# Two chunked scans of a hybrid transformer block: preparing the next tile during the levels of this one, beta in the decay, small blocks in the second scan's first levels

## The reference, cut to what matters

```python
# gated delta rule, per chunk (g: cumulated log decay)
decay = exp(where(incl, g[..., :, None] - g[..., None, :], -inf))
k_beta = k * beta[..., None]
a = where(strict, einsum('bhntd,bhnsd->bhnts', k_beta, k) * decay, 0.0)
rhs = concatenate([v * beta[..., None], k_beta * exp(g)[..., None]], -1)
sol = triangular_solve(a + eye(C), rhs, lower=True, unit_diagonal=True)   # -> u, w
qk = einsum('bhntd,bhnsd->bhnts', q, k) * decay
v_new = u - w @ S
o = (q * exp(g)) @ S + qk @ v_new
S = S * exp(g_last) + (k * exp(g_last - g)).T @ v_new

# second scan: the decay G is a vector over the 128 key features
dec = exp(where(tri, G[:, :, :, None, :] - G[:, :, None, :, :], -inf))
A = einsum('bhtd,bhsd,bhtsd->bhts', q, k, dec)
o = (q * exp(G)) @ S + A @ v
S = exp(G_last) * S + (k * exp(G_last - G)).T @ v
```

## Time and profile before

| | |
|---|---|
| median of 3 runs | 3026.27 us (3025.71 to 3035.88) |
| profiled execution | 3025.89 us, its span 3024.0 us |
| busy | PE 2452.7 us (81%), its weight loads 1330.1 (44%), DVE 1006.4 (33%), ACT 476.1 (16%), POOL 330.2 (11%) |
| mean granted clock of PE | 0.894 of full speed (2.4 GHz) |
| DMA | 540.71 MB, 179 GB/s over the span |
| first scan | about 555.7 to 850 us |
| second scan | about 2106 to 2349 us |

### The profile page before, as it was taken

How to read it: one execution, slowest core, us unless ns; L and a number is a source line. 1 busy time by engine, 2 the same in 40 slices (tenths; PEclk the granted TensorE clock), 3 DMA queues, 4 the chain that set the end, 5 groups by cost and what they waited for, 6 DMA issues and landing times. The chain is left out here.

```text
span 3024.0 us, 37725 instructions
## 1 busy us (share of the span) xinstructions
PE 2452.7 (81%) x15432; PEld 1330.1 (44%) x15432; DVE 1006.4 (33%) x2009; ACT 476.1 (16%) x942; POOL 330.2 (11%) x388
## 2 busy tenths in 40 slices
PE   5888998767679599999998696898466848898896
PEld 2346565667558222222222374567365632222221
DVE  0034432465635322222221308200768341212213
ACT  1213112211120100000000106202221110000000
POOL 0000000233300010011010000000356000000000
PEclk9999998677679799999999799999678879999997
DMA  7400114200042399999999211011000329999995
GB/s 257 157 28 22 29 42 166 100 2 2 3 146 98 115 339 348 346 339 341 346 356 358 70 48 65 28 56 56 0 1 1 140 77 389 409 409 410 409 410 235
DMA packets 165552, 540.71 MB, mean 179 GB/s; under 512 B 14512, under 2 KB 49712, under 8 KB 158896
## 3 DMA queue, kind: packets, MB, share of 16 engines
q1 hardware_dynamic: 149920, 492.93, 43.0%
q0 software_dynamic: 6144, 20.98, 2.5%
q10 hardware_dynamic: 9360, 24.96, 2.3%
HBM read 520.48 MB, written 18.35 MB: 178 GB/s over the span
## 5 line engine op out<-in xcount | busy, mean ns | idle before, releaser
L2238 PE MATMUL bank<-ring,arena 128*64 128x512 f32 x1024 | 265.8, 628 | 10.2 <-ACT arena L2294 9.7
L2194 PE MATMUL bank<-ring,arena 128*64 128x512 f32 x1024 | 244.1, 597 | 21.7 <-DMA ring<-in_moe_w_up_dram 21.7
L2179 PE MATMUL bank<-ring,arena 128*64 128x512 f32 x1024 | 249.5, 608 | 10.7 <-DMA ring<-in_moe_w_gate_dram 9.5
L451 PE MATMUL bank<-arena,ring 128*128 128x384 f32 (+1 forms) x704 | 245.0, 511 | 2.7 <-ACTq L2538 1.5
L451 PEld LDWEIGHTS bank<-arena,ring 128*128 128x128 f32 x704 | 134.8, 192 | 111.5 <-issue 33.9
L481 PE MATMUL bank<-ring,arena 128*128 128x256 f32 (+1 forms) x800 | 170.4, 375 | 6.9 <-ACTq L2538 6.9
L442 DVE COPY arena<-bank 128x384 f32<-128x384 f32 (+4 forms) x60 | 30.3, 505 | 424.0 <-PE bank L451 231.8
L2345 DVE TENSOR_TENSOR arena<-arena,bank 128x512 f32<-128x512 f32 x32 | 21.9, 685 | 423.7 <-PE bank L2205 292.1
L481 PEld LDWEIGHTS bank<-ring,arena 128*128 128x128 f32 x800 | 151.1, 201 | 26.8 <-ACTq L2538 7.5
L1622 PE MATMUL bank<-arena 128*128 128x128 f32 x608 | 108.9, 340 | 53.4 <-POOL arena L1709 31.1
L2194 PEld LDWEIGHTS bank<-ring,arena 128*64 128x64 f32 x1024 | 70.7, 137 | 180.1 <-issue 121.7
(11 more groups left out here) (346 smaller groups left out, 3256.7 us busy)
## 6 DMA issues: line engine op xcount, KB each, us to landing
ring<-in_moe_w_gate_dram SPq DMA_DIRECT2D x128, 1024.0 KB, 8.3
ring<-in_moe_w_up_dram SPq DMA_DIRECT2D x128, 1024.0 KB, 9.1
ring<-in_moe_w_down_dram SPq DMA_DIRECT2D x128, 1024.0 KB, 10.5
ring<-in_w_mod_dram SPq DMA_DIRECT2D x48, 1024.0 KB, 6.9
ring<-in_odd_w_in_dram SPq DMA_DIRECT2D x16, 1024.0 KB, 5.6
ring<-in_even_w_in_dram SPq DMA_DIRECT2D x10, 1024.0 KB, 11.7
ring<-in_even_w_out_dram SPq DMA_DIRECT2D x4, 1024.0 KB, 12.3
tok_lat_dram<-X ACTq DMA_DIRECT2D x8, 512.0 KB, 2.9
```

What stands on the lines that cost most here:

```text
L451: mm = nc.tensor.matmul(bk[:, 0:b_ - a], lhs(k), rhs(k, a, b_), start=k == 0, stop=k == kb - 1)
L2179: mm = nc.tensor.matmul(G_[half(hf), :], xl[:, k, :], columns(g, kk, hf), start=k == 0, stop=k == KB - 1)
L2194: mm = nc.tensor.matmul(U_[half(hf), :], xl[:, k, :], columns(u, kk, hf), start=k == 0, stop=k == KB - 1)
L2238: mm = nc.tensor.matmul(D_[half(hf), :], HT[:, f % 4, half(f // 4)], columns(c, kk, hf), start=f == 0, stop=f == KB - 1)
```

## The change

In the first scan, the preparation of tile n+1 is spread over the levels and joins of tile n: decay sums after level 3, logs before and between the joins, exponentials on ACT after each direction's `W64`, key-key products after the joins, mask and first blocks after those. `QE` has two buffers; the one not in use holds the block masks `BT`. Beta moves from the keys into the decay: `ETM` is multiplied by beta in the instruction that masks it, per head; the keys for the update carry beta through `ELB`. The right side is formed before the inverse: keys times state (level 1), times exp(g), minus values (`RH`); one product with the inverse then gives minus v_new, which ACT copies with scale -1. The state's update becomes one instruction per head.

In the second scan, the gates of tile n+1 are made (in place, in `ZT`) at the start of tile n on ACT, the outputs of tile n stand on PE between levels 1 and 2 of tile n+1 and its state update on DVE after level 2's growth. Levels 0 to 5 multiply only the diagonal 32x32 blocks, which are gathered in a compact `ATC`; the last two levels multiply the off-diagonal blocks; ACT puts `AT` together. Fourteen full level masks and two strict masks leave the constants.

```diff
-    nc.vector.tensor_tensor(BEG, BETA, EG, ALU.mult)
+    nc.vector.tensor_tensor(ELB, BETA, EL, ALU.mult)
...
+    def decay_sums(n, d):
+        if n:
+            nc.tensor.wait_ge(gd["attn"], 2 * (n - 1) + d + 1)
+        sums_at_queries(bk(d, 3), tile(n, d)[0], d).then_inc(gd["sums"], 1)
+
+    def key_pairs(n, d):
+        cols = tile(n, d)[1]
+        nc.tensor.wait_ge(gd["exps"], 2 * n + d + 1)
+        each_head(bk(d, 3), lambda h: KT[:, h, cols], lambda h: KT[:, h, cols]).then_inc(gd["kk"], 1)
+
+    def key_states(n, d):
+        cols = tile(n, d)[1]
+        if n:
+            nc.tensor.wait_ge(gd["done"], 2 * (n - 1) + d + 1)
+        else:
+            nc.tensor.wait_ge(gd["zero"], 1)
+        each_head(bk(d, 1), lambda h: KT[:, h, cols], lambda h: S[d][:, h, :]).then_inc(gd["ks"], 1)
+
+    def query_pairs(n, d):
+        cols = tile(n, d)[1]
+        nc.tensor.wait_ge(gd["rh"], 2 * n + d + 1)
+        each_head(bk(d, 1), lambda h: KT[:, h, cols], lambda h: QT[:, h, cols]).then_inc(gd["kq"], 1)
...
+            if l == 2:
+                for d in range(2):
+                    query_pairs(n, d)
...
+            if l == 3 and n < NT - 1:
+                for d in range(2):
+                    decay_sums(n + 1, d)
...
+        if n < NT - 1:
+            for d in range(2):
+                key_pairs(n + 1, d)
...
+            each_head(bk(d, 1), lambda h: TT[d][:, h, :], lambda h: RH[d][:, h, :]).then_inc(gd["vnp"], 1)
...
+                nc.tensor.matmul(o, QE[d][n % 2][:, h, :], S[d][:, h, :], start=True, stop=False)
                 nc.tensor.matmul(o, QK[d][:, h, :], VN[d][:, h, :], start=False, stop=True)
...
+    def decay_exps(n, d):
+        first = (slice(0, CHUNK), slice(CHUNK, P))[d]
+        second = (slice(0, CHUNK), slice(CHUNK, P))[1 - d]
+        qe = QE[d][n % 2]
+        nc.scalar.wait_ge(gd["diff"], 2 * n + d + 1)
+        nc.scalar.activation(qe[:, :, second], qe[:, :, second], ACT.Exp)
+        nc.scalar.activation(qe[:, :, first], heads(bk(d, 3)[:, :])[:, :, first], ACT.Exp)
+        nc.scalar.activation(ETM[d], ETM[d], ACT.Exp).then_inc(gd["exps"], 1)
...
             nc.scalar.activation(W64[d][far, :, :], half64(d, 2)[far, :, :], ACT.Copy).then_inc(gd["ucopy"], 1)
+            if n < NT - 1:
+                decay_exps(n + 1, d)
...
+            nc.scalar.wait_ge(gd["vnp"], 2 * n + d + 1)
+            nc.scalar.activation(VN[d], heads(bk(d, 1)[:, :]), ACT.Copy, scale=-1.0).then_inc(gd["vncopy"], 1)
...
-            nc.gpsimd.wait_ge(gd["exps"], 2 * n + d + 1)
-            nc.gpsimd.tensor_tensor(QE[d], QE[d], QT[:, :, tile(n, d)[1]], ALU.mult).then_inc(gd["qe"], 1)
         for l in range(1, 5):
             for d in range(2):
                 if l == 1:
                     nc.gpsimd.wait_ge(gd["atc"], NB * (2 * n + d + 1))
-                nc.gpsimd.tensor_tensor(BT[d][l], ATC[d], small_mask(d, l), ALU.mult).then_inc(gd["bt"], 1)
+                    if n:
+                        nc.gpsimd.wait_ge(gd["out"], 2 * (n - 1) + d + 1)
+                nc.gpsimd.tensor_tensor(BT[d][n % 2][l], ATC[d], small_mask(d, l), ALU.mult).then_inc(gd["bt"], 1)
...
+            nc.gpsimd.tensor_tensor(KL[d], heads(KTOK[:, tile(n, d)[0], :]), gcol(ELB, d, tile(n, d)[0]),
+                                    ALU.mult).then_inc(gd["kl"], 1)
+        if n < NT - 1:
+            for d in range(2):
+                decayed_queries(n + 1, d)
...
+        nc.vector.wait_ge(gd["sums"], 2 * n + d + 1)
+        dv(nc.vector.tensor_tensor(ETM[d][:, :, halves[0]], sums[:, :, halves[0]], scal(PAIR1), ALU.add))
+        dv(nc.vector.tensor_tensor(ETM[d][:, :, halves[1]], sums[:, :, halves[1]], scal(PAIR2), ALU.add))
+        dv.then(nc.vector.tensor_tensor(QE[d][n % 2][:, :, halves[1]], sums[:, :, halves[1]], scal(TOT1), ALU.add))
+        nc.vector.tensor_scalar(ETM[d], ETM[d], 0.0, None, ALU.min).then_inc(gd["diff"], 1)
+
+    def decay_of(n, d):
+        tl = tile(n, d)[0]
+        nc.vector.wait_ge(gd["exps"], 2 * n + d + 1)
+        for h in range(H):
+            dv(nc.vector.scalar_tensor_tensor(ETM[d][:, h, :], ETM[d][:, h, :], col(BETA, d, tl, h), C(f"incl{d}"),
+                                              ALU.mult, ALU.mult))
+
+    def first_blocks(n, d):
+        nc.vector.wait_ge(gd["kk"], 2 * n + d + 1)
+        dv.settle()
+        for i in range(NB):
+            nc.vector.tensor_tensor(ATC[d][blk(i), :, :], heads(bk(d, 3)[:, :])[blk(i), :, blk(i)], ETM[d][blk(i), :, blk(i)],
+                                    ALU.mult).then_inc(gd["atc"], 1)
+        nc.vector.wait_ge(gd["atc"], NB * (2 * n + d + 1))
+        dv.then(nc.vector.tensor_tensor(TTC[d], ATC[d], small_mask(d, 0), ALU.mult))
+        dv.then(nc.vector.tensor_tensor(TTC[d], ident32, TTC[d], ALU.subtract))
+        nc.vector.transpose(TC[d].rearrange("p h c -> p (h c)"), TTC[d].rearrange("p h c -> p (h c)")).then_inc(gd["tc"], 1)
...
+    def right_sides(n, d):
+        tl = tile(n, d)[0]
+        nc.vector.wait_ge(gd["ks"], 2 * n + d + 1)
+        for h in range(H):
+            ins = nc.vector.scalar_tensor_tensor(RH[d][:, h, :], heads(bk(d, 1)[:, :])[:, h, :], col(EG, d, tl, h),
+                                                 heads(VTOK[:, tl, :])[:, h, :], ALU.mult, ALU.subtract)
+        ins.then_inc(gd["rh"], 1)
...
+            if l == 1:
+                for d in range(2):
+                    right_sides(n, d)
...
+        if n < NT - 1:
+            decay_logs(n + 1, 0)
...
+        if n < NT - 1:
+            decay_logs(n + 1, 1)
...
+        if n < NT - 1:
+            for d in range(2):
+                decay_of(n + 1, d)
+            for d in range(2):
+                first_blocks(n + 1, d)
...
+            for h in range(H):
+                ins = nc.vector.scalar_tensor_tensor(S[d][:, h, :], S[d][:, h, :], col(ET, d, tl, h),
+                                                     heads(bk(d, 1)[:, :])[:, h, :], ALU.mult, ALU.add)
+            ins.then_inc(gd["done"], 1)
...
+    def outputs(n):
...
             nc.tensor.wait_ge(hg["turncopy"], HG_0 + g + 1)
             if n == 0 and d == 0:
                 nc.tensor.wait_ge(hg["zero"], HG_0 + 1)
+            if n:
+                nc.tensor.wait_ge(hg["done"], HG_0 + g - 1)
...
+                nc.tensor.wait_ge(hg["whole"], HG_0 + 2 * (n - CT) + d + 1)
                 nc.tensor.wait_ge(hg["qfin"], HG_0 + 2 * (n - CT) + d + 1)
...
+                    nc.tensor.matmul(o, QF[d][:, h, :], S[d][:, h, :], start=True, stop=False)
                     nc.tensor.matmul(o, AT[d][:, h, :], heads(HV[:, tl, :])[:, h, :], start=False, stop=True)
+            for h in range(H):
+                mm = nc.tensor.matmul(heads(bk(d, 3)[:, :])[:, h, :], KRT[d][:, h, :], heads(HV[:, tl, :])[:, h, :],
+                                      start=True, stop=True)
+            mm.then_inc(hg["out"], 1)
...
+    def level(n, l):
+        for d in range(2):
+            lat = tile(n, d)[2]
+            keys = KS[n % 2][d] if l < 2 else KC[d]
+            queries = HQ[:, :, lat] if l == 0 else QC[d]
...
+            if l < NSM:
+                if l >= 2:
+                    nc.tensor.wait_ge(hg["att"], HG_0 + at_small(n, l - 2, d))
+                elif n > CT:
+                    nc.tensor.wait_ge(hg["att"], HG_0 + at_small(n - 1, NSM - 2 + l, d))
+                if l == 1:
+                    nc.tensor.wait_ge(hg["turncopy"], HG_0 + 2 * (n - 1) + d + 1)
+                for h in range(H):
+                    for i in range(NB):
+                        mm = nc.tensor.matmul(compact(d, l)[blk(i), h, :], keys[:, h, blk(i)], queries[:, h, blk(i)],
+                                              start=True, stop=True)
...
+    for n in range(NT):
+        if is_lat(n):
+            level(n, 0)
+            level(n, 1)
+        if n:
+            outputs(n - 1)
+        if is_lat(n):
+            for l in range(2, NL):
+                level(n, l)
+        for d in range(2):
...
+            z, ks = decays(n, d), KS[n % 2][d]
+            if n > 1:
+                nc.scalar.wait_ge(hg["fin"], HG_0 + 2 * (n - 2) + d + 1)
+                if is_lat(n - 2):
+                    nc.scalar.wait_ge(hg["att_used"], HG_0 + at_level(n - 2, 1, d))
+            ac(nc.scalar.activation(ks, z, ACT.Sigmoid, scale=-1.0))
+            ac(nc.scalar.activation(z, z, ACT.Sigmoid))
...
+    for n in range(NT):
+        if n < NT - 1:
+            gates(n + 1)
...
+                nc.scalar.wait_ge(hg["att"], HG_0 + at_small(n, NSM - 1, d))
+                for i in range(NB):
+                    nc.scalar.activation(AT[d][blk(i), :, blk(i)], ATC[d][blk(i), :, :], ACT.Copy)
+                nc.scalar.wait_ge(hg["att_used"], HG_0 + at_level(n, NL - 1, d))
+                for s_, t_ in pairs32(d):
+                    nc.scalar.activation(AT[d][blk(s_), :, blk(t_)], heads(bk(d, 0)[:, :])[blk(s_), :, blk(t_)], ACT.Copy)
```

(55 more changed lines are left out.)

350 lines of the change are left out of this document (140 added, 210 removed).

## The result

The changed kernel takes 2904.15 us (median of 4 runs, 2898.86 to 2907.63); the kernel before, beside it, 3028.26. The ratio is 0.9585, 95% interval 0.9561 to 0.9608: 124 us less. Forecast were 2915 us (2887 to 2955), 111 less. The profiled execution of after took 2898.86 us, its span 2896.8, at a mean granted clock of 0.902; 127 us less than the one of before.

What follows compares the result with a forecast made beforehand. It took both scans to be bound by chains of short dependent steps, with no engine full. Savings of 62 (first scan), 47 (second) and 2 (constants), 111 us off the profiled 3025.9, gave 2915 us, range 2887 to 2955.

Steps and rivals of the forecast that it cites:

- clock 1.00 in levels 1 and 2: First scan, sign in the profile after: PE at its full granted clock in these levels, priced 4.6 and 4.4 us.
- "Issue" gaps: First scan levels: PE stands with both operands ready, read as instruction stream falling behind; one of 0.9 us a tile kept.
- (c): First scan: VectorE's per-head instructions cost 0.41 or more, VectorE becomes the bound; 17 us lost, 2932 us; chance 0.12.
- The added 1.7: First scan joins: decay logs on VectorE +1.1, exponentials on ACT +0.6; 7.3 becomes 9.0 us.
- Start: First scan: no wait for POOL's memsets and scaling, no turn; the first level comes 6 us earlier.
- all at half: First scan bound: PE at the half clock throughout, 47.5 us a tile, saving 9 us.
- X: Second scan, end of direction 0's last growth in a latent tile; outputs forecast from X+8.9, POOL's level 2 at X+17.1.
- floor of 3.8: Second scan level: POOL and VectorE take turns, 1.9 us a direction, so never under 3.8; 3.85 taken for 4.02.
- (a): Both scans: the clock stays at its full level throughout; 134 us saved, 2892 us; chance 0.12.
- (b): Both scans: PE's clock stays low and PE bounds both; first scan -9, second -38, 2977 us; chance 0.14.
- (e): Second scan: small blocks do nothing, levels stay at 4.02; 34 us saved there instead of 47, 2928 us; chance 0.1.
- (d): Slower than before: in-order queues hold next-tile work ahead of this tile's chain; about 3041 us; chance 0.02.

Runs made afterwards that it cites:

- the serial kernel: The changed kernel with the first scan's overlap undone, each tile's preparation issued at its own start; 2958.52 us, ratio 0.9767.
- the three kernels with the old masks: The kernel before (3028.26 us), and it with only the new first scan (2969.62 us) or only the new second scan (2971.58 us).

## Why the prediction was right

**First scan, 62 for 62.** From first level product to first level product the five periods are 38.09, 36.92, 37.76, 38.08 and 36.62 us, mean 37.5; forecast 37.2. The terms, as means: levels 16.9 (17.1), joins 9.1 (9.0), key pairs and inverse product 5.9 (5.3), outputs to the next level 5.5 (5.8). The mechanism was right. That the sum came out to the us is in part luck, since terms missed in both directions:
- Within the levels errors cancelled. The query products pulled level 2 to 5.6 us instead of 4.4, as PE ran them at half the clock: "clock 1.00 in levels 1 and 2" held for level 1. Level 3 took 3.3 instead of 4.4 in the tile shown.
- "Issue" gaps: forecast one of 0.9 a tile from the earlier trace rows. After has 10.6 us over six tiles on the two lines of level products, 1.8 a tile, where before had 16.5, 2.8 a tile. The reading as an instruction stream that falls behind is borne out by the records of DMA packets: in the tile shown, packets of 16 KB of the kind "instruction" land at 643.91, 649.27 and 653.20, and PE goes on at 645.23, 650.67 and 654.71. All 15 such gaps of PE in this scan end 1.2 to 1.6 us behind such a landing, and all 21 in the scan before; of 35 landings the other 20 in after are followed by no gap.
- Per-head instructions from PSUM: 0.26 from start to start, under the lower bound 0.28; I took 0.32. Rival (c) fell. The decay's two SBUF inputs made it 0.38 (3.0 us where the sum has 2.4, beside PE's dense stretch), and 0.53 in the serial kernel, where POOL ran beside it for part of the time.
- Joins: the 9.0 came out by luck. The added 1.7 was 0.5 too little (2.2 measured), and the 7.3 that it was added to 0.3 too much (a bare 6.97 in the serial kernel).
- Key pairs: priced at half clock, and the inverse product at full; the clock came back later, at 670, 5 us into the stretch. 0.6 low.
- Start: the first level came 12.2 us into the scan instead of 16.7, 4.5 earlier and not 6. L1408 of direction 0, beside POOL's memsets, took 1.99 us and the one of direction 1 behind them 0.43; the walk had not counted that. The last tile gave it back: from its first level product to the end of the scan 32.5 us instead of the 38.3 before, 5.8 less where the sum has 4.

Two slips in the recorded sums decide nothing: the bound "all at half" is 5 x 0.2 + 10 = 11 us of saving and not 9, and 2142.5 + 30.5 is 2173.0 and not 2171.7, so that the second scan's own terms give 46 and not 47.

**Second scan, 56 for 47.** The walk held step by step: VectorE idle at the tile's start, outputs from X + 8.3 (8.9), level 2 at X + 16.8 (17.1), states in it. Three terms were too dear. Levels: 3.62, not 3.85, over 4.5 levels, and less handing over, 1.4 a tile. States 3.25, not 3.9, and level 2 in all 0.6. The end of the context tiles came 34.3 us into the scan, forecast 36.3. The three latent tiles behind the first, 35.8, 36.6 and 37.1 instead of 39 (the earlier trace rows had 47.45), make 7.5 of the 9 us, the context tiles 2.

The term that was mis-sized is the level, with its floor of 3.8. I summed full durations, 0.73 + 0.62 on POOL and 0.28 twice on VectorE per direction. But alone, POOL's products start 0.68 apart, and one of the four growths (0.41) runs while POOL waits for VectorE. The Trainium skill, SBUF — State Buffer, § Terms (shared port pair), says that the loser stands still for the whole instruction. The rows agree: a growth of 0.42 takes 0.83 beside POOL (1.05 in the earlier trace rows), a product of 0.73 takes 0.91 beside VectorE. That a level couldn't go under 3.8 was my arithmetic with durations, not the page's; the trace has 3.62.

**Constants, 0.8 for 2.** The last w_mod chunk is used at 41.70 to 41.85 in the three kernels with the old masks and at 39.80 to 41.46 (median 40.9) in the others. It is inside the bounds and too small for a median.

**Rivals.** (a): the clock's mean rose from 0.71 to 0.79 in the first scan, not to 1.00, and fell from 0.76 to 0.61 in the second. There PE waits for POOL in every level, so a slower PE shows only in the outputs. (b): in the second scan its condition held and its price didn't: outputs at half clock for direction 0 only. (e) is answered in part: at the steady level the last 0.7 us of copy saved bought nothing; undoing the 32-wide products wasn't tried. (d) had no sign. What decided the total being 2904 and not 2915 is the second scan's 9 us; the rest is scatter outside the scans.

## What to carry to other kernels

- Work moved into another stage's idle time is worth its own length only if the stage has room on every engine it touches: here 11.6 us of preparation came off a tile for 2.2 more in the joins and 2.3 more in PE's last stretch. Nearly all of the saving was the overlap; the shorter chain alone left a steady tile as long as it was.
- Put a block of products into the gaps of the steps around it, by heads, if another engine's next step waits for PE's queue and not for the block: 4 to 5 us a tile here, for the same instructions.
- Read slack off the durations too: an instruction that takes twice its usual time beside another engine is a wait, and takes up added work for nothing.

## What the runs showed of the hardware

- VectorE's SCALAR_TENSOR_TENSOR of 128x128 with one input in PSUM, one in SBUF and a scalar column is 0.34 us long and starts every 0.26 us in a row; by its length it would have been dearer than the 0.28 of the plain one in the earlier trace rows, by its spacing it isn't.
- In runs of 32x32 products PE can stand for instructions: all 36 "issue" gaps over 0.25 us in the first scan of before and after (18.1 and 13.6 us in sum, joins and other lines included) end 1.2 to 1.6 us behind the landing of a 16 KB instruction packet.
- The same first scan, instruction for instruction, took 228.0 to 233.9 us. The joins of the first four tiles were equal to 0.02 us; the differences are in the levels (15.5 to 18.1) and key pairs with inverse products (4.9 to 6.4), where the granted clock changes at other moments.
